# Differential attention: a unit's maxima ahead of the previous unit's combination on VectorE, its scores ahead of the transposes on TensorE

## The chip, the cores and the metric

One core of a Trainium2 chip runs the whole program. The metric is the device time of one execution in microseconds (us); the median of several runs is compared. A core has a tensor engine (TensorE, PE in the rows, with PEld for its weight loads), a vector engine (VectorE, DVE), a scalar engine (ScalarE, ACT), GpSimd (POOL) and a queue of DMA issues (SyncE, SP). Each engine works through its own list of instructions in order; semaphores are all that ties one list to another.

## What is computed

A two-layer transformer trunk: 1,024 tokens of x and 256 of context, width 1,024. The change touches one stage of the first layer, the differential attention. Cut to what matters, for each of 4 heads:

```python
s1 = einsum('qd,kd->qk', q1, k1) * scale          # head size 64
s2 = einsum('qd,kd->qk', q2, k2) * scale
p = softmax(s1) - lam * softmax(s2)
o = einsum('qk,kd->qd', p, v)                      # value size 128
```

The tokens of x look at all 1,280 keys, those of the context at the 256 context keys alone. Before and after it stand projections, a convolution, a second attention (MLA, 16 heads) and two feed-forward stages, all in fp32, the large products as exact sums of split operands.

## The kernel before

`diff_attention` (L2259 on) works on units. A unit is 128 queries of one head: 8 full units against 1,280 keys and 2 short ones (the context's) against 256, for 4 heads, so `ALL` = 40 units. Two units make a pair (`QP` = 2), and a pair's product with the values is taken at once.

A unit passes through these steps:

- `scores(n, half)` on TensorE (L2514 and L2515): six matmuls for a full unit's half, into `s_ps`. There is one `s_ps` buffer of three banks for each half, so the scores of a half wait for the previous unit's exponential of that half.
- `maxima(n)` on VectorE (L2446): one reduction for each half.
- `exponentials(n)` on ScalarE (L2405): for each half the exponential with the maximum as bias, and its row sum.
- `combine(n)` on VectorE (L2454, L2456, L2460): reciprocals of both sums, a factor, then e1 + factor * e2 over the row. It waits for both exponentials.
- `turned(n, at)` on TensorE (L2530, L2534): up to three groups of transposes (four key tiles, four, and two with the reciprocal), each into one of the two banks of `t_ps`. The first group waits for `combine(n)`.
- `turn_copy(n)` on ScalarE (L2417): each group is copied to `pt`.
- `product(pair)` on TensorE (L2545): ten key tiles of values, into the same two banks in turn.
- `output(pair)` on VectorE (L2468), after which GpSimd stores it.

Every fill of `t_ps` (a group of transposes, a product, or a window, below) goes to the bank that is not the last one's. `free(f)` makes fill f wait until fill f-2 was read. Every fourth unit (n % 4 == 2) TensorE also computes a piece of the modulation vectors, 64 matmuls into the same banks (`m.product`, L165), and VectorE adds a bias to it (`m.add`, L177). It is called a window below.

The lists of the engines, in the kernel before, for each n:

- TensorE, iteration n: first transposes of n, first scores of n+2, second transposes of n, second scores of n+2, third transposes of n, then (n odd, from 3 on) the product of the pair n-3, n-2, then (n % 4 == 2) the window.
- VectorE, iteration n: `combine(n)`, `maxima(n+1)`, the output of the product that TensorE's iteration n-1 made, the bias of iteration n-1's window.
- ScalarE: the two exponentials of unit n+1, then the three copies of unit n.

Of the kernel before, what the change touches and what calls it, by code (L numbers as in the profile page):

```python
# [2258 lines left out]
def diff_attention(nc, head, joined, o_heads, qk, v_rows, ident, silu, mod, ada_w, ada_b, ada_first):  # L2259
# [10 lines left out]
    ALL = B_HEADS * NU  # L2270
# [7 lines left out]
    def unit(n):  # L2278
        return UNITS[n % NU]

    def groups(n):
        first = unit(n)[1]
        return [list(range(a, min(a + 4, KT))) for a in range(first, KT, 4)]
# [4 lines left out]
    def window(n):  # L2288

        g = n // ADA_EVERY  # L2290
        return g if n % ADA_EVERY == 2 and g < ADA_GROUPS else None

    def pair_at(n):

        p = (n - QP - 1) // QP
        return p if n % QP == 1 and 0 <= p < ALL // QP else None
# [18 lines left out]
    with ExitStack() as ctx:  # L2315
# [111 lines left out]
        @block.vector  # L2427
        def _(dve):
            m.clear(dve)

            for a in range(2):
                dve.tensor_tensor_reduce(lam_prod[:, a, :], lam_t[:, 2 * a, :], lam_t[:, 2 * a + 1, :], 1.0, 0.0,
                                         ALU.mult, ALU.add, lam_small[:, a:a + 1]).then_inc(s.lam_step.sem, 1)
            dve.wait_ge(s.lam_exp.sem, 1)
            dve.tensor_tensor(lam_small[:, 4:5], lam_small[:, 3:4], lam_small[:, 2:3], ALU.subtract)\
               .then_inc(s.lam_step.sem, 1)
            dve.wait_ge(s.lam_step.sem, 3)
            dve.tensor_scalar(lam_small[:, 5:6], lam_small[:, 4:5], -LAMBDA_INIT, None, ALU.add)\
               .then_inc(s.lam_done.sem, 1)
            dve.wait_ge(s.lam_done.sem, 1)  # L2440

            def maxima(n):
                first = unit(n)[1] * P
                for half, full, mx in ((0, s.s1_full, s.max1), (1, s.s2_full, s.max2)):
                    dve.wait_ge(full.sem, n + 1)
                    dve.tensor_reduce(stats[:, n % 4, NEG_MAX + half:NEG_MAX + half + 1], s_ps[:, half, first:T], AX.X,  # L2446
                                      ALU.max, negate=True).then_inc(mx.sem, 1)

            def combine(n):
                first, st = unit(n)[1] * P, stats[:, n % 4, :]  # L2450
                a, b = e1[:, n % 3, first:T], e2[:, n % 2, first:T]
                dve.wait_ge(s.exp1.sem, n + 1)
                dve.wait_ge(s.exp2.sem, n + 1)
                dve.reciprocal(st[:, INVERSE:INVERSE + 2], st[:, SUMS:SUMS + 2]).then_inc(s.inverse.sem, 1)  # L2454
                dve.wait_ge(s.inverse.sem, n + 1)
                dve.scalar_tensor_tensor(out=st[:, FACTOR:FACTOR + 1], in0=st[:, INVERSE + 1:INVERSE + 2],  # L2456
                                         scalar=lam_small[:, 5:6], in1=st[:, SUMS:SUMS + 1], op0=ALU.mult,
                                         op1=ALU.mult).then_inc(s.factor.sem, 1)
                dve.wait_ge(s.factor.sem, n + 1)
                dve.scalar_tensor_tensor(out=a, in0=b, scalar=st[:, FACTOR:FACTOR + 1], in1=a, op0=ALU.mult,  # L2460
                                         op1=ALU.add).then_inc(s.p_done.sem, 1)

            def output(pair):
                dve.wait_ge(s.o_full.sem, pair + 1)
                if pair >= 2:

                    dve.wait_ge(o_stored[pair % 2].sem, 16 * (pair // 2))
                dve.tensor_tensor(o_t[:, pair % 2, :], t_ps[:, product_fill[pair] % 2, 0:QP * P], pt[:, pair % 2, KT, :], ALU.mult)\  # L2468
                   .then_inc(s.o_out.sem, 1)

            maxima(0)
            for n in range(ALL + QP + 1):
                if n < ALL:
                    combine(n)
                if n + 1 < ALL:
                    maxima(n + 1)
                if n and pair_at(n - 1) is not None:
                    output(pair_at(n - 1))
                if n and window(n - 1) is not None:
                    m.add(dve, window(n - 1))  # L2480
# [14 lines left out]
        @block.tensor  # L2495
        def _(pe):
            def scores(n, half):
                u, first = unit(n)
                j = n // NU % 2
                full, exp = ((s.s1_full, s.exp1), (s.s2_full, s.exp2))[half]  # L2500
                if n == 0 and half == 0:
                    pe.wait_ge(head.loaded, 16 * head.LOADS)
                elif n % NU == 0 and half == 0:

                    pe.wait_ge(qk_in[j].sem, 16 * head.LOADS * (n // NU // 2 + j))
                if n:

                    pe.wait_ge(exp.sem, n)
                q = q_st[j][:, half, u * P:(u + 1) * P]
                for a, width in chunks:  # L2510
                    if a + width <= first * P:
                        continue
                    keys = slice(a, a + width)
                    pe.matmul(s_ps[:, half, keys], q, k_hi[j][:, half, keys], start=True, stop=False)  # L2514
                    mm = pe.matmul(s_ps[:, half, keys], q, k_lo[j][:, half, keys], start=False, stop=True)  # L2515
                mm.then_inc(full.sem, 1)

            def free(f):

                if f >= 2:  # L2520
                    sem, value = released[f - 2]
                    pe.wait_ge({"t_copied": s.t_copied, "o_out": s.o_out, "row_done": s.row_done}[sem].sem, value)

            def turned(n, at):
                f, group = turn_fills[n][at], groups(n)[at]
                if at == 0:
                    pe.wait_ge(s.p_done.sem, n + 1)
                free(f)
                for g, kt in enumerate(group):
                    mm = pe.transpose(t_ps[:, f % 2, g * P:(g + 1) * P], e1[:, n % 3, kt * P:(kt + 1) * P],  # L2530
                                      ident[:, :])
                if group[-1] == KT - 1:
                    g = len(group)
                    mm = pe.transpose(t_ps[:, f % 2, g * P:(g + 1) * P],  # L2534
                                      stats[:, n % 4, INVERSE:INVERSE + 1].broadcast_to([P, P]), ident[:, :])
                mm.then_inc(s.t_full.sem, 1)

            def product(pair):
                h, first, f = pair // PAIRS, unit(pair * QP)[1], product_fill[pair]
                if pair % PAIRS == 0:  # L2540
                    pe.wait_ge(v_in[h % 2].sem, 16 * (h // 2 + 1))
                free(f)
                pe.wait_ge(s.t_copied.sem, copies_before[pair * QP + QP - 1])
                for kt in range(first, KT):
                    mm = pe.matmul(t_ps[:, f % 2, 0:QP * P], v[:, h % 2, kt, :], pt[:, pair % 2, kt, :],  # L2545
                                   start=kt == first, stop=kt == KT - 1)
                mm.then_inc(s.o_full.sem, 1)

            for half in range(2):
                scores(0, half)  # L2550
            for half in range(2):
                scores(1, half)
            for n in range(ALL + QP):
                for at in range(3):
                    if n < ALL and at < len(groups(n)):
                        turned(n, at)
                    if n + 2 < ALL and at < 2:
                        scores(n + 2, at)
                if pair_at(n) is not None:
                    product(pair_at(n))  # L2560
                if window(n) is not None:
                    free(ada_fill[window(n)])
                    m.product(pe, window(n))
# [2031 lines left out]
```

## Time and profile before

| | us |
|---|---|
| median of 3 runs (3316.13 to 3322.68) | 3317.86 |
| the profiled execution | 3314.38 |
| its span in the profile | 3312.6 |
| the attention stage in it | about 351 to 620 |
| granted TensorE clock, mean of the span | 0.982 of full |

Over the span TensorE is busy 3162.3 us (95%), VectorE 1942.9 (59%), ScalarE 1412.6 (43%), GpSimd 551.0 (17%). Times of rows are us from the span's start. A row of the timeline gives the start, the duration, the engine, the line, what is written and read, the number of instructions merged in it (x), and in brackets how long the engine had been idle and what ended that. The duration of a matmul row reaches past the start of the next row, since matmuls overlap: a step's length is read from start to start.

### The profile page before, as it was taken

What the parts mean: (1) busy time and instruction counts of PE and PEld (TensorE: products, weight loads), DVE (VectorE), ACT (ScalarE), POOL (GpSimd) and SP (SyncE); (2) the same over time, 40 slices, a digit from 0 to 9 for tenths busy, and PEclk for the clock granted to TensorE, in tenths of its full rate; (3) what the DMA queues carried; (4) which work ended last, traced back from release to release, by engine and by line L of the source; (5) the groups of instructions that cost most, each with busy time, mean ns of one, the idle gap of its engine ahead of it and who ended that gap; (6) DMA issues with size and microseconds to landing.
All of it is one profiled execution on the core that took longest, in us unless ns stands there. A gap on an engine that the chain in (4) does not pass through costs nothing. (4 is left out here: it accounts for less than half of the span.)

```text
span 3312.6 us, 47976 instructions
## 1 busy us (share of the span) xinstructions
PE 3162.3 (95%) x19172; PEld 2728.8 (82%) x19172; DVE 1942.9 (59%) x2362; ACT 1412.6 (43%) x2445; POOL 551.0 (17%) x688
## 2 busy tenths in 40 slices
PE   7999798899999999999998999999999899999998
PEld 5888677788999999888787778888887778888886
DVE  4999666556755665444444335555555676776344
ACT  5121456465333333344365325555554533333333
POOL 0001000121222222020022101111111233332000
PEclk8999999899999999999999999999999999999999
DMA  6224685533122122556434642422222322222654
GB/s 215 70 91 155 201 260 215 174 102 84 55 77 76 57 77 77 176 182 184 141 135 150 241 156 57 112 48 62 48 44 75 86 80 80 83 80 93 195 185 134
DMA packets 265389, 398.47 MB, mean 120 GB/s; under 512 B 88456, under 2 KB 189512, under 8 KB 264144
## 3 DMA queue, kind: packets, MB, share of 16 engines
q1 hardware_dynamic: 253328, 351.35, 34.7%
q0 software_dynamic: 11840, 44.06, 3.6%
q8 instruction: 153, 2.51, 0.3%
q14 instruction: 68, 0.56, 0.1%
HBM read 301.19 MB, written 94.13 MB: 119 GB/s over the span
## 5 line engine op out<-in xcount | busy, mean ns | idle before, releaser
L2100 DVE TENSOR_TENSOR ring_lo<-raw_rows,ring_hi 128x512 fp32r<-128x512 f32 x220 | 151.5, 689 | 290.6 <-ACT ring_hi L1925 290.4
L1960 DVE TENSOR_TENSOR ring_lo<-raw_rows,ring_hi 128x512 fp32r<-128x512 f32 x205 | 187.1, 913 | 203.5 <-ACT ring_hi L1850 203.1
L1925 ACT ACTIVATE ring_hi<-raw_rows 128x512 fp32r<-128x512 f32 x220 | 137.1, 624 | 333.4 <-PE banks L90 164.6
L1270 PE MATMUL banks<-y_hi,ring_hi 128*128 128x384 f32 (+2 forms) x676 | 219.1, 324 | 16.0 <-DVEq L1948 10.4
L1272 PE MATMUL banks<-y_hi,ring_lo 128*128 128x384 f32 (+2 forms) x676 | 218.8, 324 | 0.0
L1271 PE MATMUL banks<-y_lo,ring_hi 128*128 128x384 f32 (+2 forms) x676 | 218.7, 323 | 0.0
L4289 DVE TENSOR_REDUCE mla_neg_max<-mla_scores 128x1 f32<-128x1280 f32 x128 | 190.2, 1486 | 48.5 <-PE mla_scores L90 48.5
L4259 ACT ACTIVATE mla_e<-mla_scores,mla_neg_max 128x1280 f32<-128x1280 f32 x128 | 169.9, 1327 | 113.0 <-DVE mla_neg_max L4289 113.0
L4203 PE MATMUL mla_turned<-ident,mla_e 128*128 128x128 f32 x1280 | 206.3, 275 | 1.9 <-ACT mla_pt L4267 1.3
L1270 PE MATMUL banks<-differences,ring_hi 128*128 128x512 f32 (+2 forms) x572 | 196.9, 344 | 6.3 <-DVE ring_lo L1960 2.5
L1272 PE MATMUL banks<-differences,ring_lo 128*128 128x512 f32 (+2 forms) x572 | 196.5, 343 | 0.0
L1271 PE MATMUL banks<-differences,ring_hi 128*128 128x512 f32 (+2 forms) x572 | 196.4, 343 | 0.0
L4203 PEld LDWEIGHTS mla_turned<-ident,mla_e 128*128 128x128 f32 x1280 | 156.1, 140 | 48.2 <-issue 11.8
L853 DVE SCALAR_TENSOR_TENSOR ab_work<-ab_work,ab_taps 128x1295 f32<-128x1295 f32 x120 | 188.0, 1568 | 3.3
L4267 ACT ACTIVATE mla_pt<-mla_turned 128x512 f32<-128x512 f32 (+1 forms) x256 | 124.1, 485 | 119.5 <-PE mla_turned L4207 78.3
L1850 ACT ACTIVATE ring_hi<-raw_rows 128x512 fp32r<-128x512 f32 x205 | 128.4, 626 | 102.7 <-PE accs L1272 57.2
L1270 PE MATMUL accs<-y_hi,ring_hi 128*128 128x512 f32 (+1 forms) x460 | 163.6, 356 | 3.9 <-DVE ring_lo L3324 2.5
L4297 DVE COPY mla_pt<-mla_turned 128x512 f32<-128x512 f32 x128 | 87.8, 686 | 131.2 <-PE mla_turned L4203 131.0
L1272 PE MATMUL accs<-y_hi,ring_lo 128*128 128x512 f32 (+1 forms) x460 | 163.6, 356 | 0.0
L1271 PE MATMUL accs<-y_lo,ring_hi 128*128 128x512 f32 (+1 forms) x460 | 163.5, 355 | 0.0
L4221 PE MATMUL mla_turned<-mla_pt,ckv 128*64 128x128 f32 x2560 | 153.9, 275 | 1.5 <-DVE mla_pt L4297 0.8
L4221 PEld LDWEIGHTS mla_turned<-mla_pt,ckv 128*64 128x64 f32 x2560 | 138.5, 137 | 10.5 <-DVE mla_pt L4297 2.0
(474 smaller groups left out, 8792.9 us busy)
## 6 DMA issues: line engine op xcount, KB each, us to landing
raw_rows<-in_ffn_w_down SPq DMA_DIRECT2D x110, 512.0 KB, 3.6
raw_rows<-in_ffn_w_up SPq DMA_DIRECT2D x88, 512.0 KB, 3.6
da_ada_w<-in_ada_w SPq DMA_DIRECT2D x10, 4096.0 KB, 13.6
scratch_act<-conv_lines SPq DMA_DIRECT2D x22, 512.0 KB, 4.0
scratch_act<-out_raw SPq DMA_DIRECT2D x22, 512.0 KB, 4.6
out_raw<-scratch_act SPq DMA_DIRECT2D x44, 256.0 KB, 2.6
ab_raw<-in_ab_w_in SPq DMA_DIRECT2D x20, 512.0 KB, 4.0
sums<-scratch_act SPq DMA_DIRECT2D x44, 192.0 KB, 3.1
```

Source lines behind the costliest of these rows:

```text
L853: dve.scalar_tensor_tensor(out=out, in0=src[:, j:j + SPAN], scalar=taps[:, i, j:j + 1], in1=out, op0=ALU.mult, op1=ALU.add)\
L1270: pe.matmul(out, w_hi[:, w], b_hi[:, a:a + n], start=start and k == 0, stop=False, skip_group_check=True)
L1271: pe.matmul(out, w_hi[:, w], b_lo[:, a:a + n], start=False, stop=False, skip_group_check=True)
L1272: mm = pe.matmul(out, w_lo[:, w], b_hi[:, a:a + n], start=False, stop=k == KD // 2 - 1, skip_group_check=True)
L1850: act.activation(blocks(begun.hi(r)), source(r), ACT.Copy).then_inc(s.w_hi, weight(r))
L1925: act.activation(begun.hi(r), down_raw(j)[:, i * BANK:(i + 1) * BANK], ACT.Copy).then_inc(s.down_hi, 1)
L1960: dve.tensor_tensor(blocks(begun.lo(r)), source(r), blocks(begun.hi(r)).bitcast(F32), ALU.subtract)\
L2100: dve.tensor_tensor(begun.lo(r), down_raw(j)[:, i * BANK:(i + 1) * BANK], begun.hi(r).bitcast(F32), ALU.subtract).then_inc(s.down_lo, 1)
L4203: mm = pe.transpose(t_ps[:, f % 2, m * P:(m + 1) * P], e[:, n % E_SLOTS, kt * P:(kt + 1) * P], ident[:, :])
L4221: mm = pe.matmul(t_ps[half * C_V:(half + 1) * C_V, f % 2, 0:P], v[:, h % 2, kt, :], pt[:, pair % 2, half, kt, :], start=kt == 0, stop=kt = ...
L4259: act.activation(e[:, n % E_SLOTS, :], s_ps[:, n % 2, 0:T], ACT.Exp, bias=neg_max[:, n:n + 1], accum_out=sums[:, n:n + 1]).then_inc(s.exp. ...
L4289: dve.tensor_reduce(neg_max[:, n:n + 1], s_ps[:, n % 2, 0:T], AX.X, ALU.max, negate=True)\
```

## The change

Two pairs of calls are swapped. On VectorE, iteration n takes `maxima(n+1)` first and `combine(n)` after it. On TensorE, each piece of the scores of unit n+2 stands ahead of the group of transposes of unit n that it used to follow: scores, transposes, scores, transposes, transposes. No instruction is added or removed; the buffers, the waits that each instruction carries and the lists of ScalarE, GpSimd and SyncE are the same.

```diff
             maxima(0)
             for n in range(ALL + QP + 1):
+                if n + 1 < ALL:
+                    maxima(n + 1)
                 if n < ALL:
                     combine(n)
-                if n + 1 < ALL:
-                    maxima(n + 1)
                 if n and pair_at(n - 1) is not None:
                     output(pair_at(n - 1))
...
             for n in range(ALL + QP):
                 for at in range(3):
+                    if n + 2 < ALL and at < 2:
+                        scores(n + 2, at)
                     if n < ALL and at < len(groups(n)):
                         turned(n, at)
-                    if n + 2 < ALL and at < 2:
-                        scores(n + 2, at)
```

## Rows read from the trace of the kernel before

**Rows 1.** Stretches: us, then busy us of each engine, granted clock, DMA.

```profile
358.00:610.00 252.00, 226.94 (x1657) 183.62 (x1658) 169.40 (x221) 147.60 (x259) 18.74 (x33) 0.99 0.72 234
```

**Rows 2.** Waits of TensorE's weight loads, 358 to 612: us, times, longest.

```profile
PEld da_scores L2514 <- ACT da_e L2405: 26.0, 18, 2.4
```

**Rows 3.** Timeline, 366 to 373, before the first product; VectorE, ScalarE, TensorE.

```profile
366.43 2.88 DVE L2446 TENSOR_REDUCE da_stats<-da_scores 128x1 f32<-128x1280 f32 x2
...
370.86 0.17 DVE L2454 RECIPROCAL da_stats<-da_stats 128x2 f32<-128x2 f32 x1 [1.55 <-ACT da_e L2405]
...
372.79 2.88 DVE L2446 TENSOR_REDUCE da_stats<-da_scores 128x1 f32<-128x1280 f32 x2
...
367.95 1.33 ACT L2405 ACTIVATE da_e<-da_scores,da_stats 128x1280 f32<-128x1280 f32 x1 [1.02 <-DVE da_stats L2446]
...
372.93 0.66 PE L2530 MATMUL da_turned<-ident,da_e 128*128 128x128 f32 x4 [0.15 <-DVE da_e L2460]
```

**Rows 4.** Timeline, 390 to 400: a pair without a window, from product to product.

```profile
390.55 0.60 PE L2530 MATMUL da_turned<-ident,da_e 128*128 128x128 f32 x4
...
390.75 0.42 DVE L2468 TENSOR_TENSOR out_heads_out<-da_turned,da_pt 128x256 f32<-128x256 f32 x1 [2.36 <-PE da_turned L2545]
...
390.91 0.48 PE L2514 MATMUL da_scores<-da_first_k_hi,da_first_q 128*128 128x512 f32 x1
...
392.15 0.60 PE L2530 MATMUL da_turned<-ident,da_e 128*128 128x128 f32 x4
...
392.79 0.60 ACT L2417 ACTIVATE da_pt<-da_turned 128x512 f32<-128x512 f32 x1 [0.94 <-PE da_turned L2530]
...
393.00 2.88 DVE L2446 TENSOR_REDUCE da_stats<-da_scores 128x1 f32<-128x1280 f32 x2
...
393.75 0.38 PE L2530 MATMUL da_turned<-ident,da_e 128*128 128x128 f32 x2
...
394.08 0.60 PE L2530 MATMUL da_turned<-ident,da_e 128*128 128x128 f32 x4
...
394.28 0.49 ACT L2417 ACTIVATE da_pt<-da_turned 128x384 f32<-128x384 f32 x1 [0.89 <-PE da_turned L2534]
...
394.67 1.32 ACT L2405 ACTIVATE da_e<-da_scores,da_stats 128x1280 f32<-128x1280 f32 x1
...
396.13 0.50 PE L2514 MATMUL da_scores<-da_first_k_hi,da_first_q 128*128 128x512 f32 x1 [1.45 <-ACT da_e L2405]
...
399.32 2.97 PE L2545 MATMUL da_turned<-da_pt,da_v 128*128 128x256 f32 x13
```

**Rows 5.** Timeline of TensorE, 427 to 439: a pair with a window.

```profile
427.36 0.60 PE L2530 MATMUL da_turned<-ident,da_e 128*128 128x128 f32 x4
...
430.97 3.66 PE L165 MATMUL da_turned<-da_ada_w,silu 128*32 128x256 f32 x64
434.56 0.66 PE L2530 MATMUL da_turned<-ident,da_e 128*128 128x128 f32 x4
...
438.14 1.03 PE L2545 MATMUL da_turned<-da_pt,da_v 128*128 128x256 f32 x4
```

**Rows 6.** Timeline, 403 to 406: a full unit's transposes among short scores, then a window.

```profile
403.64 0.60 PE L2530 MATMUL da_turned<-ident,da_e 128*128 128x128 f32 x4
...
405.67 3.66 PE L165 MATMUL da_turned<-da_ada_w,silu 128*32 128x256 f32 x64
...
404.34 1.74 ACT L2417 ACTIVATE da_pt<-da_turned 128x512 f32<-128x512 f32 x3 [0.60 <-DVE out_heads_out L2468]
```

**Rows 7.** Stretches (columns as in rows 1) and two timeline rows of TensorE: the clock.

```profile
446.00:450.00 4.00, 3.54 (x12) 3.06 (x13) 2.38 (x5) 2.50 (x6) 0.00 (x0) 0.57 1.02 410
...
574.00:578.00 4.00, 1.84 (x5) 1.46 (x6) 2.41 (x4) 3.30 (x5) 0.00 (x0) 0.78 0.70 284
...
446.46 0.73 PE L2514 MATMUL da_scores<-da_k_hi,da_q_stacked 128*128 128x512 f32 x1 [2.19 <-ACT da_e L2405]
...
451.24 1.03 PE L2545 MATMUL da_turned<-da_pt,da_v 128*128 128x256 f32 x4
```

## The prediction

> **What bounds the kernel now.** I read the stretch of the attention stage first, since nothing outside it is touched. There TensorE is busy 226.9 of 252 us, VectorE 169.4, ScalarE 147.6 [rows 1]. So at most about 25 us, 0.8% of the kernel, can be won without taking work away. The waits say where they are: TensorE's weight loads for the scores wait 18 times for ScalarE's exponential, 26.0 us in all [rows 2]. These gaps are the whole prize; what the reader is to see is that they are not spread over all 40 units but come at few places.
>
> The timeline tells which loop makes them. Before the first product a unit takes 6.36 us, from one pair of maxima at 366.43 to the next at 372.79 [rows 3]: maximum, 1.52 us later the first exponential, about 1.40 later the second, 1.5 later the reciprocal (VectorE idle 1.55 until then), 1.93 later the next maxima. This is a chain of VectorE and ScalarE in turn, and the change cuts it, since the maxima of n+1 no longer stand behind the combination of n. Once products run, the picture is another. From the end of one product (390.55, where the next transposes start) to the start of the next is 8.77 us, of which TensorE idles 1.45, before 396.13 [rows 4]; a pair with a window takes 3.61 + 3.59 + 3.58 = 10.78 and has no such gap [rows 5].
>
> **The prices, by row.** A step is read from start to start. Scores of a half 1.24, four transposes 0.36 (390.55, 390.91, 392.15), the third group 0.33 (393.75 to 394.08). From the end of a transpose group (392.51) to its copy 0.28, or 0.2 for the third; a copy takes 0.6 and the third is followed by the exponential after 0.39 (394.28, 394.67). From the first exponential's start to the scores that wait for it 1.46 (394.67, 396.13) [rows 4]. From the reciprocal to the transposes that wait for the combination 2.07 [rows 3]. A copy that ends at 404.34 + 0.57 x 2 + 0.06 = 405.54 releases the window at 405.67, 0.13 later: copies of the second group are already what is late when little stands between the groups [rows 6]. No step is longer or shorter after the change; all its effect is in the order.
>
> **Edit on TensorE.** Before, the scores' second half (1.24 us) stands between the second and the third transposes of a unit. So the second copy is over long before the bank is wanted. After, the second and third groups are adjacent, and product or window behind them need the bank of the second group. Take the end of a product as 0. After the change: scores to 1.24, transposes to 1.60, scores to 2.84, transposes to 3.20, third group to 3.52. The second copy runs 3.48 to 4.08, the third starts at 4.08, and what fills the next bank starts at 4.08 + 0.13 = 4.21 instead of 3.6 [rows 4 to 6]. This is a new wait of 0.6 to 0.7 us ahead of every product and window of full units. Queued behind that wait is all of TensorE's list, the next scores too.
>
> The same order delays the exponentials. ScalarE's list has those of n+2 behind the three copies of n, so the first cannot start before 4.08 + 0.39 = 4.47, and the scores of n+3 start at 5.93. Before it was 396.13 - 390.55 = 5.58 [rows 4]. The gap in front of them grows from 1.45 to 2.4 us, because the first transposes of n+1, which ran ahead of the gap, now stand behind the scores.
>
> **Edit on VectorE.** The maxima of n+2 can start when their scores are over, at 1.24 + 0.2 = 1.44 (0.2 is also what the output, 390.75, needs after a product), and the exponential could go at 2.96. It waits for ScalarE's list until 4.47. So what the cut chain gives is taken by the copies. The combination of n+1 stands behind both maxima (start 4.4, end 6.5); the transposes that need it come at 7.2, so this is hidden by 0.7 us. Without that cover TensorE would pay the difference. The outputs and the bias of a window move behind nothing new that is late: the combination ahead of them is over before the product is (12.4 against 14.5). No DMA of another queue is moved past; a store follows its output as before.
>
> **The sum, against the profiled execution.** I went through all 40 units like this.
> - Pairs of full units without a window, 4-5, 20-21, 24-25: 5.93 + 4.21 = 10.15 instead of 8.77, +1.38 each, +4.1.
> - With a window, 10-11, 14-15, 30-31, 34-35: twice the wait of 0.6, +1.24 each, +5.0.
> - Pairs whose new scores are short, 6-7 and 26-27: window at 2.37 instead of 405.67 - 403.64 = 2.03 [rows 6], and as much before the product, +0.7 each. In 16-17 and 36-37 the combination stands later by about 0.5. Together +2.4.
> - 12-13 and 32-33: here the product ahead is that of a short pair, so the chain has no cover, and the loop of 5.93 competes with the old one. From 438.14 to 451.24 it took 13.10 [rows 5, 7]; after, 1.72 + 5.93 + 4.21 = 11.87. -1.2 each, -2.5. In 22-23, likewise half covered, +0.2.
> - The start, units 0 to 3: the first combination comes 2.9 later (behind maxima that wait for scores), then the loop runs at 5.93 instead of 6.36, then window and product pay their waits. -0.6.
> - 8-9, 18-19, 28-29 and the last units: within 0.1 each, -0.2.
>
> Sum +8.4 us with the clock always at 2.4 GHz.
>
> **The clock.** After two of the five gaps of 2.2 us the granted clock fell to its lower level, 1.2 GHz, in part of the next stretch (means of 0.57 and 0.78) [rows 7]. The price: from the scores at 446.46 to the product 4.78 us, where it is 3.19 in 396.13 to 399.32, so 1.6 each [rows 4, 7]. The sum above has taken the two falls of before away (they are in 13.10). After the change seven gaps of about 2.4 us remain by my schedule; at two in five that is two to three falls, +4.0. Bounds are none (0) and seven (+11.2). Total +12.4: 3314.4 + 12.4 = 3326.8. The median of the runs is 3.5 above the profiled execution, so 3330 there.
>
> The Trainium skill, Perfetto Trace Analysis, "Matmuls", asks that independent groups rotate through different PSUM banks so that the evacuation of one overlaps the next group's matmuls. In this trace that rotation works because scores fill the time of a copy. By that rule nothing changes, as the rotation is kept, and the sum would be near the first rival's.
>
> **Rivals.**
> 1. The copies cost nothing: the bank's wait is covered, because the window or product lies in TensorE's queue anyway. For it: in rows 5 no such wait is seen. Against it: rows 6 show one already with 0.3 us between the groups. It would take about 15 us off (8 windows at 0.6, 15 products at 0.7): 3330 - 15 = 3315, no change.
> 2. Faster: the maxima win. If the copies are over about 1.1 us earlier than I place them (by 2.96 + the start of the exponential), ScalarE's list holds nothing back, and the scores of n+3 start at 4.42, not 5.93, in seven places: -10.6, on top of rival 1, and with gaps below 1 us no fall of the clock, -4.0. 3315 - 14.6 = 3300. It decides at the third copy's start, 4.08 against 2.96. The gaps of rows 2 speak for it as a prize; the order of ScalarE's list, in which these copies come first, speaks against it.
> 3. The clock falls after each of the seven gaps: 8.4 + 11.2 = 19.6, 3337.5. For it: the gaps are longer than before. Against: three of five gaps of 2.2 us did nothing.
> 4. The change does nothing that is measured, the new loop paying exactly for the waits: near rival 1's time.
>
> **Chances.** Forecast 0.60 (3326 to 3334), rival 1 with rival 4 0.20, rival 2 0.09, rival 3 0.11. Within 0.2%, 6.6 us, is about what a measurement of this kernel can tell from no change; the forecast's own lower edge (no falls, +8.4, some waits shorter) touches it, so 0.04 of it goes to no change. Slower 0.67, same 0.24, faster 0.09. The range leaves rival 2 out and takes in the others: 3315 to 3338.
>
> **What would show it.** In the new profile: the waits of products (L2545) and windows (L165) for ScalarE's copy (L2417), hardly there before, at 0.6 to 0.7 us each and some 15 us in all; the gap ahead of scores near 2.4 us in unwindowed pairs, at 5.93 from the product's end; in the first units 5.93 from scores to scores; VectorE's combination behind the maxima with no transposes waiting for it except at the start. The stage should be 8 to 16 us longer and all else the same. The prediction is wrong if the first exponential starts right at its maximum (then rival 2), or if windows still start 3.6 us after a product (then rival 1).

## The result, and the profile after

The changed kernel takes 3324.78 us (median of 17 runs), the kernel before 3316.70 beside it: a ratio of 1.0024, 95% interval 1.0018 to 1.0030, so 6 to 10 us (0.18% to 0.30%) slower. The profiled execution has a span of 3323.7 us, 11.1 over the one of before.

The stretch of the stage, as in rows 1 (columns there). TensorE's granted clock is 0.97 of full on average; it was 0.99:

```profile
358.00:620.00 262.00, 231.94 (x1651) 186.21 (x1650) 174.05 (x221) 144.76 (x260) 18.80 (x33) 0.97 0.69 225
```

Waits of TensorE's weight loads from 358 to 625 us of the changed kernel: us in total, times, longest. The first line answers rows 2.

```profile
PEld da_scores L2514 <- ACT da_e L2405: 27.0, 16, 2.3
PEld da_turned L2545 <- ACT da_pt L2417: 5.7, 11, 0.6
PEld da_turned L165 <- ACT da_pt L2417: 4.2, 8, 0.6
```

The waits for the exponential are what they were, 27.0 us against 26.0. Those of products (L2545) and windows (L165) for ScalarE's copy have grown, from 2.1 us in 6 waits to 9.9 us in 19. The kernel before, 358 to 612 us:

```profile
PEld da_turned L2545 <- ACT da_pt L2417: 1.4, 4, 0.4
PEld da_turned L165 <- ACT da_pt L2417: 0.7, 2, 0.4
```

A pair without a window, from the end of a product (527.92, where the next scores start) to the next product, is this in the timeline of the changed kernel; it answers rows 4:

```profile
527.92 0.58 PE L2514 MATMUL da_scores<-da_first_k_hi,da_first_q 128*128 128x512 f32 x1
528.31 0.42 DVE L2468 TENSOR_TENSOR out_heads_out<-da_turned,da_pt 128x256 f32<-128x256 f32 x1 [2.32 <-PE da_turned L2545]
...
529.96 0.60 ACT L2417 ACTIVATE da_pt<-da_turned 128x512 f32<-128x512 f32 x1 [3.34 <-PE da_turned L2530]
...
530.88 0.82 PE L2530 MATMUL da_turned<-ident,da_e 128*128 128x128 f32 x6
...
531.51 0.98 ACT L2417 ACTIVATE da_pt<-da_turned 128x512 f32<-128x512 f32 x2 [0.96 <-PE da_turned L2530]
...
532.38 1.33 ACT L2405 ACTIVATE da_e<-da_scores,da_stats 128x1280 f32<-128x1280 f32 x1
532.49 0.15 DVE L2454 RECIPROCAL da_stats<-da_stats 128x2 f32<-128x2 f32 x1
...
533.85 0.51 PE L2514 MATMUL da_scores<-da_first_k_hi,da_first_q 128*128 128x512 f32 x1 [2.05 <-ACT da_e L2405]
...
538.01 0.48 PE L2545 MATMUL da_turned<-da_pt,da_v 128*128 128x256 f32 x1 [0.36 <-ACT da_pt L2417]
```

The second and third groups of transposes are one row now (x6, plus the transpose of the reciprocal). Their copies run at 531.51, the exponential behind them starts at 532.38, 4.46 after the product's end, and the scores at 533.85, 5.93 after it. The product starts at 538.01: 10.09 instead of 8.77. The idle time in brackets is shorter than the wait, since the previous matmul's modelled end reaches into it.

A pair with a window, TensorE alone; it answers rows 5 (from product's end, 432.49, to window, to next product):

```profile
436.73 3.66 PE L165 MATMUL da_turned<-da_ada_w,silu 128*32 128x256 f32 x64 [0.36 <-ACT da_pt L2417]
...
444.47 0.70 PE L2545 MATMUL da_turned<-da_pt,da_v 128*128 128x256 f32 x2 [0.36 <-ACT da_pt L2417]
```

The window starts 4.24 after the product's end (3.61 before), the next product at 11.98 (10.78 before).

The clock of the changed kernel in four stretches, as in rows 7. Behind the start-up these are the only places of this stage where it falls:

```profile
360.00:364.00 4.00, 2.49 (x8) 2.03 (x8) 3.43 (x5) 2.84 (x4) 0.00 (x0) 0.71 1.02 410
374.00:378.00 4.00, 3.12 (x11) 2.77 (x12) 2.45 (x2) 2.22 (x5) 0.00 (x0) 0.67 1.03 219
398.00:402.00 4.00, 3.43 (x12) 2.98 (x13) 2.65 (x2) 2.42 (x5) 0.00 (x0) 0.65 0.22 66
586.00:590.00 4.00, 4.00 (x17) 3.44 (x16) 1.82 (x2) 1.55 (x3) 0.00 (x0) 0.62 0.11 43
```

Each of them is called a fall below. The first comes in units 0 and 1, after a wait of 1.5 us before 361.60. The other three follow gaps of 2.1 us ahead of scores (before 374.88, 398.57 and 585.70); four more such gaps (before 369.05, 452.00, 505.93 and 533.85) are followed by none.

### The profile page after: what moved, and what is told of

The parts are those of the page before. It is cut to its first block and busy times, and to the rows that moved or that the text cites. A ratio compares the mean times of both kernels' runs of the same rounds, so it can differ in the third digit from the quotient of the medians.

```text
span 3323.7 us, 47976 instructions
## 1 busy us (share of the span) xinstructions
PE 3173.9 (95%) x19172; PEld 2737.8 (82%) x19172; DVE 1946.6 (59%) x2362; ACT 1410.0 (42%) x2445; POOL 553.0 (17%) x688
```

## The experiments

Three theories went in. A: the order on TensorE costs, through the second copy. B: the later combination on VectorE costs. C: the clock costs. Two more, D and E, came from the results.

**The two edits apart.** First the TensorE edit alone, on the kernel before:

```diff
                 for at in range(3):
+                    if n + 2 < ALL and at < 2:
+                        scores(n + 2, at)
                     if n < ALL and at < len(groups(n)):
                         turned(n, at)
-                    if n + 2 < ALL and at < 2:
-                        scores(n + 2, at)
```

> The change's TensorE edit alone; VectorE keeps the combination ahead of the maxima. Theory A (the second and third transposes now adjacent, so that product and window wait 0.6 to 0.7 us for the second copy, and ScalarE's list delays the next exponential): the pairs are as in the changed kernel (a pair without a window from product's end to next product's start 10.1 us, not 8.8; a windowed pair 12.0, not 10.8), and only where no product covers the chain is the old loop of 6.3 us there in place of 5.9. Total 8 + 2.7 = about 11 us over the kernel before. Theory B (the loss comes from the combination that stands later on VectorE, the TensorE order is harmless): within 2 us of the kernel before. Theory C (the loss is the clock's): as many us as 1.6 times the number of falls more than before, pairs at full clock unchanged.

Measured: 3331.57 us, ratio 1.0042 (1.0028 to 1.0056), 9 to 19 us slower. By the median that is more than both edits together, though the intervals touch (5 runs here). Where no product covers the chain, the timeline has this (VectorE, ScalarE, TensorE):

```profile
451.75 2.88 DVE L2446 TENSOR_REDUCE da_stats<-da_scores 128x1 f32<-128x1280 f32 x2
451.98 0.98 ACT L2417 ACTIVATE da_pt<-da_turned 128x512 f32<-128x512 f32 x2 [0.95 <-PE da_turned L2530]
...
453.27 1.33 ACT L2405 ACTIVATE da_e<-da_scores,da_stats 128x1280 f32<-128x1280 f32 x1 [0.32 <-DVE da_stats L2446]
...
454.74 0.50 PE L2514 MATMUL da_scores<-da_k_hi,da_q_stacked 128*128 128x512 f32 x1 [2.47 <-ACT da_e L2405]
```

The exponential waits 0.32 for its maximum here, which stood behind the combination; scores follow scores after 454.74 - 448.47 = 6.27 us, where the changed kernel needs 5.84 (446.16 to 452.00). Theory B falls: the combination stands where it stood, and the loss is there. The VectorE edit is worth about 4 to 6 us, by the stages' lengths (285.1 against 280.5 and 281.0, below) and the ratios, but only beside the TensorE edit. One of the four falls in this profile is twice as long, 1.6 us of the stages' difference; the rest agrees with the 2.7 expected.

The VectorE edit alone:

```diff
             for n in range(ALL + QP + 1):
+                if n + 1 < ALL:
+                    maxima(n + 1)
                 if n < ALL:
                     combine(n)
-                if n + 1 < ALL:
-                    maxima(n + 1)
```

> The change's VectorE edit alone; TensorE keeps transposes ahead of scores. The first transposes of n+1 stand ahead of the scores of n+3 and now wait for a combination behind both maxima (end 6.9 us after a product, against 3.5). Theory A: 10.4 us instead of 8.8 in pairs without a window, windowed pairs unchanged at 10.8, loop before the first product 6.9 instead of 6.4, short units 1 us later each time; sum +14 us over the kernel before, and up to +22 if the gaps, now over 3 us, lower the clock. So the VectorE edit by itself loses, and TensorE's order is what keeps that loss away in the changed kernel. Theory B: about as the changed kernel, +8 us. A theory that VectorE's edit is the useful half: faster than the kernel before.

Measured: 3342.07 us, ratio 1.0072 (1.0058 to 1.0086), 19 to 29 us slower. The timeline of the pair without a window names the new wait:

```profile
458.40 0.16 DVE L2454 RECIPROCAL da_stats<-da_stats 128x2 f32<-128x2 f32 x1
...
460.45 0.66 PE L2530 MATMUL da_turned<-ident,da_e 128*128 128x128 f32 x4 [3.17 <-DVE da_e L2460]
```

TensorE idles 3.2 us in front of transposes that wait for the combination, which now starts behind both maxima. The profile has eleven stretches at the lower clock, each behind a gap of over 2 us, and the total, 24 us, is above the upper end of 22. At 1.6 us each (one is twice as long) they explain some 19 of the 31 us by which the stage is longer (299.1 against 268.3, below), where the falls of the kernel before cost 3.2. That leaves about 15 for the order, as against the 14 expected.

**The second transposes moved back.** The changed kernel with the groups not adjacent:

```diff
-                for at in range(3):
-                    if n + 2 < ALL and at < 2:
-                        scores(n + 2, at)
+                if n + 2 < ALL:
+                    scores(n + 2, 0)
+                for at in range(2):
                     if n < ALL and at < len(groups(n)):
                         turned(n, at)
+                if n + 2 < ALL:
+                    scores(n + 2, 1)
+                if n < ALL and 2 < len(groups(n)):
+                    turned(n, 2)
```

> The changed kernel with TensorE's list as: first scores, first and second transposes, second scores, third transposes. Only the second transposes move, back ahead of the second scores. Theory A: the waits of windows and of full products for the copy go (no 0.4 us gap ahead of them), scores of n+3 start 5.6 us after a product, not 5.9, pairs with a window 10.8, without 9.1. Sum 4 us under the kernel before at an equal clock, 1 us under it if the clock falls as often as in its profile; 8 to 12 us under the changed kernel. Theory B: as the changed kernel, since the combination stands where it stood. Theory C: depends on the falls alone.

Measured: 3316.25 us, ratio 1.000 (0.999 to 1.001): all of the loss is gone, and no more than that, where 1 to 4 us under the kernel before was expected. The waits of products and windows for the copy are down to 0.9 us in 5 waits. TensorE's rows from the end of a product (429.83) on:

```profile
429.83 0.58 PE L2514 MATMUL da_scores<-da_k_hi,da_q_stacked 128*128 128x512 f32 x1
...
431.17 1.04 PE L2530 MATMUL da_turned<-ident,da_e 128*128 128x128 f32 x8
...
433.63 3.66 PE L165 MATMUL da_turned<-da_ada_w,silu 128*32 128x256 f32 x64
...
440.86 0.38 PE L2545 MATMUL da_turned<-da_pt,da_v 128*128 128x256 f32 x1
```

The window stands 3.80 behind the product's end and the next product 11.03 (4.24 and 11.98 with the groups adjacent). This is the test of theory A's first half: one group of transposes is moved, the combination stands where it stood, and 8 us come back. Its profile has five falls in the stage, one more than the changed kernel's, so it isn't the clock of this stage that gave them back.

**The exponential ahead of the copies.** The changed kernel, ScalarE's list altered in seven iterations (the rest of the rewriting only splits two helpers):

```diff
+            EARLY = (0, 1, 4, 12, 20, 24, 32)
...
+                    if n and n - 1 not in EARLY:
+                        exponential(n + 1, 0)
+                    exponential(n + 1, 1)
+                for at in range(len(groups(n))):
+                    turn_copy(n, at)
+                    if n in EARLY and at == 0:
+                        exponential(n + 2, 0)
```

> The changed kernel; in the seven iterations whose gap is 2.1 us ScalarE takes the first exponential of n+2 right after the first copy of n, ahead of its second and third. Theory A (ScalarE's list, not the maximum, holds the exponential back): scores of n+3 start 4.4 to 4.5 us after a product instead of 5.9, the gap of 2.1 is 0.9, no clock fall at these places, but the first transposes of n+1 then wait for the combination (6.5 against 5.7); a pair without a window 13.7 instead of 14.3. Sum against the changed kernel: 7 falls of 1.6 and about 4 us of order, -12 to -15; against the kernel before -4 to -6. If the maximum held it: no step changes.

Measured: 3316.03 us, ratio 1.0000 (0.9991 to 1.0009) to the kernel before, 10 us under the changed kernel on the same chip. The same pair as above in its timeline (the product ends at 521.62):

```profile
524.69 1.33 ACT L2405 ACTIVATE da_e<-da_scores,da_stats 128x1280 f32<-128x1280 f32 x1 [0.43 <-DVE da_stats L2454]
...
526.01 0.97 ACT L2417 ACTIVATE da_pt<-da_turned 128x512 f32<-128x512 f32 x2
526.16 0.51 PE L2522 MATMUL da_scores<-da_first_k_hi,da_first_q 128*128 128x512 f32 x1 [0.66 <-ACT da_e L2405]
...
528.24 0.66 PE L2538 MATMUL da_turned<-ident,da_e 128*128 128x128 f32 x4 [0.66 <-DVE da_e L2468]
...
531.19 0.48 PE L2553 MATMUL da_turned<-da_pt,da_v 128*128 128x256 f32 x1 [0.36 <-ACT da_pt L2417]
```

Scores start 4.54 after the product's end, as expected, and then the transposes wait for the combination. The pair takes 13.77 us from product to product (517.42 to 531.19), expected 13.7, against 14.29 (523.72 to 538.01). So the order of ScalarE's list was what held the exponential. TensorE has no gap over 1.7 us left in the stage and the clock does not fall there after the start-up, as expected. The sum was 4 to 6 us too low against the kernel before: it took seven falls away, and the profiles of the changed kernel have four, a difference of 4.8 us.

**The clock.** The changed kernel with dummy work in its seven long gaps: transposes of the identity ("dummy turns") into a bank whose content nobody reads any more. Such a gap is called filled below.

```diff
+                if n in (0, 1, 4, 12, 20, 24, 32):
+                    f = turn_fills[n][2] + 1
+                    free(f)
+                    for g in range(12):
+                        pe.transpose(t_ps[:, f % 2, g % 4 * P:(g % 4 + 1) * P], ident[:, :], ident[:, :])
```

> The changed kernel, and in the seven places where TensorE idles 2.1 us ahead of scores it turns the identity 12 times (1.1 us) into the bank that the second copy has just left; nothing reads that. The idle time is cut into about 0.6 and 0.6 us, the scores start as before. Theory A: pairs unchanged, the clock stays at its upper level, no step of the seven is 1.6 us longer: 0 to 5 us under the changed kernel, by its number of falls in an unprofiled execution. Theory C: all of the loss of 8 us goes. If the falls don't depend on the gaps, it is no faster than the changed kernel and the profile shows 0.57 or 0.78 stretches again.

Measured: 3316.10 us, ratio 0.9998 (0.9989 to 1.0007) to the kernel before, 8.7 us under the 3324.78 of the changed kernel (by the two ratios 0.26%): more than the 0 to 5 expected. The profile has one low stretch behind the start-up instead of four; a pair without a window still takes 14.30 us (520.94 to 535.24). So the loss by order stayed, and as much was won elsewhere. By its total alone, theory C seemed to win. It says nothing yet of the kernel before, which has such gaps too. So dummy turns went into its own gaps, and into the kernel with the second transposes moved back:

```diff
+            FILLED = {0: 12, 1: 12, 2: 12, 13: 12, 33: 12, 5: 8, 9: 8, 21: 8, 25: 8, 29: 8}
...
                     if n < ALL and at < len(groups(n)):
                         turned(n, at)
+                    if at == 0 and n in FILLED:
+                        f = turn_fills[n][0] + 1
+                        free(f)
+                        for g in range(FILLED[n]):
+                            pe.transpose(t_ps[:, f % 2, g % 4 * P:(g % 4 + 1) * P], ident[:, :], ident[:, :])
                     if n + 2 < ALL and at < 2:
                         scores(n + 2, at)
```

> The kernel before, with the same dummy turns of the identity in ten of its own gaps ahead of scores (12 turns, 1.1 us, in the five of 2.2 us; 8 turns in five of 1.4 to 1.6), between the first transposes of n+1 and the scores that wait. The order of the work is untouched. Theory D, new after the filled kernel of the first call came out level with the kernel before: both kernels lose 1.6 us at nearly every gap of 2 us, the kernel before too, and the change's own order costs 8 to 9 us at an equal clock. Then this one is about 8 us (5 gaps times 1.6) under the kernel before, ratio 0.9976, and its runs scatter less. If the gaps of the kernel before mostly go by without a fall, as three of five did in its profile, it is 3 us under it. If the dummy turns help in another way than by the clock, a pair without a window is shorter than 13.1 us from product to product.

> The kernel with the second scores between the second and third transposes (0.5 us over the kernel before at an equal clock, by the stage's length in its profile less 1.6 for each of its 5 falls), with the seven gaps filled as in the filled kernel. Theory D: about 8 us under the kernel before, level with the filled kernel before within 2 us, and 8 us under the filled changed kernel, since the copy's waits are gone. Without a hold on the clock: level with the kernel before.

Measured: 3305.04 us, ratio 0.9964 (0.9952 to 0.9977), and 3308.27 us, ratio 0.9971 (0.9961 to 0.9982). Both beat both kernels. The order of the work is as it was: in the filled kernel before a pair takes 387.75 to 400.85, 13.10 us. The scores start on time behind the dummy turns:

```profile
396.19 1.32 ACT L2405 ACTIVATE da_e<-da_scores,da_stats 128x1280 f32<-128x1280 f32 x1
396.35 1.09 PE L2562 MATMUL da_turned<-ident 128*128 128x128 f32 x8
...
397.66 0.50 PE L2514 MATMUL da_scores<-da_first_k_hi,da_first_q 128*128 128x512 f32 x1 [0.22 <-ACT da_e L2405]
```

With the gaps filled in both, then, the change costs 3316.10 against 3305.04; on two chips, by their own ratios, 0.9998 against 0.9964, which is 0.34% or 11 us. The stages of the two profiles are 276.2 and 266.2 us long, each with one fall in its first units.

**Where the clock's part lies.** Four more kernels: the changed kernel and the kernel before once more, for a second profile of each, and the kernel before with fewer fills (`FILLED = {13: 12, 33: 12}` and `{0: 12, 1: 12, 2: 12, 13: 12, 33: 12}`).

> The changed kernel itself once more, beside the others on one chip: ratio 1.0024 to the kernel before as measured (1.0018 to 1.0030), stage about 281 us less or more 1.6 for each fall that it has more or fewer than 4. It is the other profile of the same program: which of its seven gaps of 2.1 us are followed by a fall shows whether that is fixed by the gap or differs from execution to execution.

> The kernel before, unchanged, once more as a kernel of its own: ratio 1.000 within 0.001, which is what the comparison itself can tell. Its new profile shows whether the falls of the clock in the stage are again the two after the 2.2 us gaps at units 13 and 33 (fixed by the place, as the four of the changed kernel were in both of its profiles) or others.

> The kernel before with the 12 dummy turns in two gaps alone, at units 13 and 33, which are the two that a fall followed in its profile. If timed executions are like the profiled one, 3.2 us (2 times 1.6) under the kernel before, ratio 0.9990, and the rest of the 11 us of the ten fills comes from elsewhere. If all of the 11 us hung on these two, 0.9965.

> The kernel before with 12 dummy turns in the five gaps of 2.2 us, none in those of 1.4 to 1.6. If a fall costs 1.6 us and comes after every gap of 2.2 us in timed executions: 8 us under the kernel before, ratio 0.9976. If the gaps of 1.4 to 1.6 us count for nothing, as in every profile so far (no fall after any of them), level with the ten fills, 11 us under, 0.9965.

Measured: 1.0024 (1.0014 to 1.0033), 1.0002 (0.9993 to 1.0010), 0.9978 (0.9968 to 0.9988), 0.9971 (0.9962 to 0.9980). Two fills give some 7 us (4 to 11), where their two falls cost 3.2. So theory D, a fall of 1.6 us at nearly every gap, falls: there is a gain that no gap of the stage holds. The second profile of the changed kernel has four falls again, three in the same places (374 to 378, 398 to 402, 586 to 590) and the first some 3 us earlier (358 to 362). The one of the kernel before has two again, one where it was (576 to 582) and one at 364 to 368, with none at 446.

I then measured each profile in two parts: the stage, from the first matmul of the scores to the last of the products, and from there to the first matmul of the second attention's scores. The listing of a tile gives first and last starts; these two rows are the changed kernel's (duration min/median/max in ns, then first and last start in us):

```profile
L2545 PE MATMUL da_turned<-da_pt,da_v x336: 377/379/483, 388.4 to 632.0; 128*128 128x256 f32 x168
...
L88 PE MATMUL mla_scores<-k_first_hi,q_first_hi x192: 362/484/792, 1986.2 to 2484.0; 96*128 96x512 f32 x128, 96*128 96x256 f32 x64
```

| kernel | stage, us | from there to the second attention, us | time against before |
|---|---|---|---|
| before, two profiles | 269.0, 267.6 | 1360.3, 1359.0 | 1 |
| changed, two profiles | 280.5, 281.0 | 1354.2, 1355.0 | 1.0024 |
| TensorE edit alone | 285.1 | 1356.1 | 1.0042 |
| VectorE edit alone | 299.1 | 1356.8 | 1.0072 |
| second transposes moved back | 274.3 | 1356.4 | 1.0000 |
| exponential first | 270.9 | 1357.0 | 1.0000 |
| changed, filled | 276.2 | 1352.9 | 0.9998 |
| before, ten, five, two fills | 266.2, 266.3, 266.1 | 1351.0, 1351.7, 1353.0 | 0.9964, 0.9971, 0.9978 |
| moved back, filled | 268.9 | 1352.6 | 0.9971 |

The stage is 12.5 us longer by the change (280.75 against 268.3), and the part behind it, in which not one instruction was changed, is 5 us shorter. The table stops at the second attention. From there to the end the two profiles of the kernel before themselves differ by 5.7 us (1332.4 and 1338.1; the changed kernel has 1337.5 and 1336.9), so the two parts of one profile don't add up to the difference of the medians.

Three things account for most of the 5 us. The first is the hand-over to the next stage, where TensorE idles 1.0 us less, 2.96 and 2.81 against 3.94 and 3.90. The kernel before, then the changed one:

```profile
624.21 1.01 PE L2759 MATMUL out_sums<-out_uo,out_ones 128*128 128x128 f32 x3 [3.94 <-DVE out_gains L3042]
```

```profile
635.34 1.01 PE L2759 MATMUL out_sums<-out_uo,out_ones 128*128 128x128 f32 x3 [2.96 <-DVE out_gains L3042]
```

The second is a wait of ScalarE for weights of the feed-forward stage: 5.22 and 5.67 us in the kernel before, 4.76 and 4.70 in the changed one, and 2.5 in the kernel with two fills:

```profile
807.38 0.63 ACT L1832 ACTIVATE ring_hi<-raw_rows 128x512 fp32r<-128x512 f32 x1 [5.22 <-DMA raw_rows<-in_ffn_w_up]
```

```profile
801.85 0.63 ACT L1832 ACTIVATE ring_hi<-raw_rows 128x512 fp32r<-128x512 f32 x1 [2.50 <-DMA raw_rows<-in_ffn_w_up]
```

All six kernels with dummy turns have 2.47 to 2.57 there, the eight profiles without them 4.66 to 5.67, whenever their stage ended. Why isn't known.

The third is the clock. Added up over this part, it is at the lower level for 63 and 64 us in the kernel before and for 58 in both profiles of the changed one. One such place, in the kernel before and in the changed one:

```profile
1824.00:1834.00 10.00, 6.20 (x21) 5.06 (x22) 2.98 (x2) 2.79 (x3) 2.12 (x4) 0.66 0.93 376
```

```profile
1836.00:1846.00 10.00, 8.49 (x43) 7.21 (x44) 4.44 (x3) 3.71 (x3) 3.01 (x6) 1.00 0.94 385
```

In one, the clock is low for most of the stretch (0.66), in the other not at all (1.00). The two stretches don't hold equal work (21 matmuls and 43). The rows of the matmul after the gap do start the same work:

```profile
1827.80 0.79 PE L88 MATMUL up_main<-up_ckv_hi,up_wkv_hi 128*128 128x512 f32 x1 [4.26 <-DVE up_out_lo L4002]
```

```profile
1837.51 0.50 PE L88 MATMUL up_main<-up_ckv_hi,up_wkv_hi 128*128 128x512 f32 x1 [2.89 <-DVE up_out_lo L4002]
```

The 18 matmuls from there on take 5.68 us (to 1833.48) and 3.60 (to 1841.11); at the lower clock a 512-column matmul follows the last after 0.43 us, at full clock after 0.23. By that, the 5 to 6 us less at the lower clock are worth an estimated 2.5.

To test whether it is the time at which the stage ends that shortens the later part (theory E), the kernel before got a delay of its own at the end of TensorE's list:

```diff
                 if window(n) is not None:
                     free(ada_fill[window(n)])
                     m.product(pe, window(n))
+            free(len(released))
+            for g in range(100):
+                pe.transpose(t_ps[:, len(released) % 2, g % 4 * P:(g % 4 + 1) * P], ident[:, :], ident[:, :])
```

> The kernel before with 100 dummy turns of the identity at the end of TensorE's list for the stage, after the last product: some 11 us in which nothing else is computed, so that all that follows starts as late as in the changed kernel, with the order inside the stage untouched. Theory E, new after the segments of the profiles (from the stage's end to the second attention 1359 to 1360 us in both profiles of the kernel before, 1354 to 1355 in both of the changed one, 1351 to 1353 in those with filled gaps): the stretches at the lower clock in later stages lie otherwise when the work before them ends at another time, and give back 4 to 5 us of the change's cost. Then this stage is 11 us longer, the part behind it about 5 us shorter (1354 to 1355), and the time 5 to 8 us over the kernel before. If later stages don't care when they start: 1359 to 1360 us there, and 11 us over the kernel before. If the part behind shrank in the changed kernel because of what its stage does, not of when it ends, the same.

Measured: 3321.02 us, ratio 1.0010 (1.0000 to 1.0019), 0 to 6 us slower. In its profile the products end at 623.9, the dummy turns run to 634.9, and the second attention starts at 1984.1:

```profile
624.07 11.08 PE L2566 MATMUL da_turned<-ident 128*128 128x128 f32 x100
636.49 1.16 PE L2762 MATMUL out_sums<-out_uo,out_ones 128*128 128x128 f32 x8 [1.33 <-DVE out_gains L3045]
```

The part behind, from the end of the dummy turns on, is 1349.2 us, 10.5 shorter than the mean of before. Of this 2.6 is the hand-over: TensorE idles 1.33 there and not 3.94, because the dummy turns lie beside what it waits for. Another 3 is ScalarE's wait for the weights, 2.47 us, as in all kernels with dummy turns. The clock is at its lower level for 51 us, 12 to 13 less than in the kernel before, an estimated 5 to 6. So the expected sign and a larger size than the 5 us expected are there, but theory E is not shown: this kernel also brings the dummy turns, and four of the kernels with fills, whose stages end between 617 and 621 us, about where the kernel before's does (620), have a part behind that is 7 to 9 us shorter too. Nor do the others follow the end of their stage: it is at 636 and 650 us with one edit alone, and their later part is longer than the changed kernel's. The stage itself was 272.6 up to the last product and not 268, with three falls behind the start-up and one in its first units: the places of the falls differ from program to program even where nothing in front of them was changed.

## Why the prediction was right

The sign, the mechanism and the range held. Point by point:

- **The wait of products and windows for the copy.** Expected at 4.21 after the product's end and 0.6 to 0.7 us long; the window is at 4.24. The profile counts 19 such waits on weight loads, where it was 6. Moving the second transposes back left 5 short ones, and took the loss away. The 15 us of the text is too much in the wait rows (9.9), which count idle time only up to the modelled ends.
- **ScalarE's list holds the exponential.** Expected 4.47 and scores at 5.93; 4.46 and 5.93. The kernel with the exponential first moved the scores to 4.54.
- **The VectorE edit is cover and loses nothing.** The combination starts 4.57 after the product's end (532.49), expected 4.4. Alone it costs some 24 us, since its cover, the scores in front of the transposes, is then missing; the text gave no price for that.
- **The terms.** A pair without a window +1.20 where no fall comes (14.29 against 13.09), expected 1.38; one with a window +1.0 (428.36 to 444.47, 16.11 us, against 423.04 to 438.14), expected 1.24. The difference is the same in both: from a product to the scores behind it are 4.13 to 4.20 us, where it was 4.32 to the transposes (386.23 to 390.55). The start, units 0 to 3, took 36.9 us against 35.3, which is 1.6 more and not 0.6 less: it holds two of the falls, 1.6 each, so the order there gave 1.6 back.
- **The clock in the stage.** Expected two to three falls after seven gaps; three came, the same in both profiles, and a fourth in the first units. Price as taken: a pair with a fall took 15.85 (388.45 to 404.30), 1.56 more than one without.
- **The sum.** Stage +12.5 us in the profiles, forecast +12.4. The order gave 2.4 less than I had added up, the clock 2.4 more; that the two cancel is luck. The filled kernels, with one fall each, agree on the order: 10.0 us (276.2 against 266.2), where the forecast at one clock was 8.4 + 3.2 = 11.6.
- **What was missing.** I took the rest of the kernel as untouched: "The stage should be 8 to 16 us longer and all else the same." It was 5 us shorter from the stage's end to the second attention, and the median rose by 8, not 12. The step that failed is the sum's last: that a stage's cost goes to the end undiminished. The forecast of 3330 is 5 too high: 4 for this reason, and 1 because the median of the kernel before, 3317.86 in 3 runs, is 3316.70 in 17. The place is shown by the two-part table and by the rows of the hand-over, the weights' wait and the clock; what sets these is open.

Rival 3 (a fall after each gap) came true for three of seven. Rival 1's time, 3315, is that of the kernel with the groups apart, 3316. Rival 2 decided where it was said to: with the exponential free of the copies the scores come at 4.5, but the transposes then wait for the combination, which the rival had left out.

Why two fills shorten the later part nearly as much as ten (1353.0 and 1351.0) is in part the weights' wait, 2.50 us in both; what makes that wait short wherever dummy turns stand in the program is open, and so is whether the time at which the stage ends moves the later low stretches. Nor can the profiles tell how many falls unprofiled executions have.

## What to carry to other kernels

With two buffers in turn, look at what stands between one writing of them and the next: work of another kind there is what hides the copy out. An order that brings the producers side by side turns that copy into a wait, also for everything behind them that needs these buffers. When a chain is cut on one engine, read the list of the next engine on it before the gain is counted: here the exponential could start 3.07 us after the product (524.69, with the copies out of its way) and started at 4.46, behind three copies. And where an engine's clock depends on its idle time, measure a change beside a kernel whose gaps are filled, or read the later stages too, before a few us are put down to the order of the work.

## What the runs showed of the hardware

Dummy turns of the identity in gaps of 1.4 to 2.2 us that TensorE had anyway made the kernel 0.36% faster, 11 us, at no cost in the order. Only some 2 us of it lie in the stage (266.2 against 268.3), the rest behind it. In the profile with two fills the granted clock stayed at 2.4 GHz in this stage after the start-up; in the two profiles of the kernel before it fell to 1.2 GHz at two places, in those of the changed kernel at four. A fall cost 1.6 us. It came after some gaps of 2.1 us and not after others of the same length (three and four of the changed kernel's). Three of the four places were the same in both profiles of the changed kernel, one of the two in those of the kernel before. The Trainium skill, TensorE: Matmul & The Clock Gate, "Why this matters for your kernels", advises against idle gaps of TensorE between bursts of matmuls because the clock falls behind them, and the gaps it means are longer than these. The runs agree in direction, though here the clock fell behind shorter ones.

What low clock costs in later stages is not fixed either. In unchanged instructions between this stage and the second attention the clock was at its lower level for 63 and 64 us in the kernel before, for 58 behind the changed stage, and for 51 to 55 in the kernels with dummy turns. For a change of 0.1 to 0.3% that is as large as the effect.
